# Order of work at the routes and gates of a two-layer diffusion trunk with product-key experts

## What is computed

```python
qr = (tb @ w_q).reshape(t, PEER_HEADS, 2, half)
s = jnp.einsum('thsk,hsnk->thsn', qr, sub_keys).astype(jnp.float32)
top_s, top_i = lax.top_k(s, PEER_TOPK)
cand_s = top_s[:, :, 0, :, None] + top_s[:, :, 1, None, :]
...
best_s, best_j = lax.top_k(cand_s.reshape(t, PEER_HEADS, PEER_TOPK * PEER_TOPK), PEER_TOPK)
gate = jax.nn.softmax(best_s, axis=-1)
act = jax.nn.gelu(jnp.einsum('td,thkd->thk', tb, expert_u[idx]).astype(jnp.float32), approximate=False)
w = (gate * act).astype(tb.dtype)
return jnp.einsum('thk,thkd->td', w, expert_v[idx])
```

## Time and profile before

| | us |
|---|---|
| median of 3 runs | 2819.0 |
| runs | 2814.79, 2819.0, 2820.88 |
| span of the profiled execution | 2820.7 |
| TensorE busy | 2637.5 (94%) |
| VectorE busy | 2261.6 (80%) |
| ScalarE busy | 1200.1 (43%) |
| GpSimd busy | 481.4 (17%) |

### The profile page before, as it was taken

The page is one execution under the profiler, slowest core; times in us unless marked ns, Lnnn a source line. Parts: engine busy times, 40 slices in busy tenths (PEclk is TensorE's granted clock), DMA queues, the critical chain, the costliest instruction groups (busy, mean ns, idle before and its releaser), DMA issues.

```text
span 2820.7 us, 48606 instructions
## 1 busy us (share of the span) xinstructions
PE 2637.5 (94%) x16753; PEld 2298.8 (81%) x16753; DVE 2261.6 (80%) x4592; ACT 1200.1 (43%) x2187; POOL 481.4 (17%) x432
## 2 busy tenths in 40 slices
PE   7999999775899999999999998989889999999998
PEld 5878877554788888888888887877879888888887
DVE  6487654996999999999999997786679888877776
ACT  5343432223954444444444445324425533333332
POOL 0000000002633333333333330000003211110010
PEclk9999999886999999999999999999999999999999
DMA  6532322643279999999999993333354599999985
GB/s 275 211 94 79 116 90 90 238 181 141 108 298 367 382 386 390 386 386 385 383 362 367 366 362 122 128 98 105 108 179 151 180 334 345 338 337 335 324 320 210
DMA packets 170928, 709.42 MB, mean 252 GB/s; under 512 B 17056, under 2 KB 48960, under 8 KB 123328
## 3 DMA queue, kind: packets, MB, share of 16 engines
q1 hardware_dynamic: 132464, 430.02, 41.3%
q0 software_dynamic: 38352, 277.92, 26.6%
HBM read 691.13 MB, written 16.65 MB: 251 GB/s over the span
## 4 chain that ended last, share of the span: by engine, by line
PE 83%; DVE 9%; DMA 3%; ACT 3%; issue 1%; SPq 0%; DVEq 0%; ACTq 0%; POOL 0%
PE ps L937 82%; DMA ring<-in_w_mod 2%; DVE hot L2685 1%; DVE hot L2680 1%; DMA gate_scratch<-spill 1%; DVE hot L2683 1%; DMA ring<-in_w_front 1%; DVE rs L2132 0%; DVE gst L2387 0%; DVE elo L2167 0%; PE ps L1085 0%; DVE loP L2232 0%; ACT hiP L1607 0%; DVE elo L2179 0%; DVE hx L2398 0%
## 5 line engine op out<-in xcount | busy, mean ns | idle before, releaser
L859 POOL DMA_INDIRECT gbuf<-in_expert_rows,gidx x192 | 277.4, 1445 | 1097.4 <-DVE yg L2738 1080.7
L937 PE MATMUL ps<-h2a,ehi 128*128 128x320 f32 x2048 | 455.0, 310 | 1.4 <-DVE elo L2695 1.4
L2084 ACT ACTIVATE ehi<-ring 128x1024 fp32r<-128x1024 f32 x256 | 271.1, 1059 | 394.5 <-PE ps L937 290.8
L2750 DVE TENSOR_TENSOR elo<-ring,ehi 128x1024 fp32r<-128x1024 f32 x256 | 313.6, 1225 | 136.2 <-ACT ehi L2084 132.9
L937 PE MATMUL ps<-ehi,wA 128*128 128x512 f32 x1280 | 375.3, 391 | 0.0
L937 PE MATMUL ps<-h2b,ring 128*128 128x192 f32 x2048 | 360.7, 327 | 1.0 <-ACT act_ahead L1969 1.0
L937 PEld LDWEIGHTS ps<-h2a,ehi 128*128 128x128 f32 x2048 | 349.3, 189 | 12.0 <-DVE elo L2695 1.9
L937 PEld LDWEIGHTS ps<-h2b,ring 128*128 128x128 f32 x2048 | 339.2, 191 | 10.6 <-issue 1.3
L937 PE MATMUL ps<-h2a,elo 128*128 128x320 f32 x1024 | 317.4, 310 | 0.0
L937 PEld LDWEIGHTS ps<-ehi,wA 128*128 128x128 f32 x1280 | 235.0, 188 | 49.8
L2728 DVE SCALAR_TENSOR_TENSOR gbuf<-gbuf,h2n 128x1024 f32<-128x1024 f32 x192 | 234.2, 1220 | 30.5 <-DMA gbuf<-in_expert_rows,gidx 25.3
(11 more groups left out here) (441 smaller groups left out, 4850.3 us busy)
## 6 DMA issues: line engine op xcount, KB each, us to landing
ring<-in_experts SPq DMA_DIRECT2D x512, 512.0 KB
ring<-in_w_mod SPq DMA_DIRECT2D x48, 1024.0 KB
ring<-in_w_side SPq DMA_DIRECT2D x24, 1024.0 KB
ring<-in_w_front SPq DMA_DIRECT2D x12, 1024.0 KB
ring<-in_w_merge SPq DMA_DIRECT2D x16, 768.0 KB
ring<-in_w_q SPq DMA_DIRECT2D x12, 1024.0 KB
gate_scratch<-spill SPq DMA_DIRECT2D x40, 256.0 KB, 2.1
gateA<-gate_scratch SPq DMA_DIRECT2D x16, 640.0 KB, 8.7
```

What stands on the lines that cost most here:

```text
L859: pool.indirect_dma_start(gbuf[:, k % 2, :], None, a[f"expert_rows{l}"], bass.IndirectOffsetOnAxis(gidx[:, at:at + 1], 0)).then_inc(gather ...
L937: return pe.matmul(out, w, x, start=start, stop=stop, **k)
L2084: act.activation(ehi[:, 2 + k % 2, :], ring[:, (u + k) % RING, DM:2 * DM], ACT.Copy).then_inc(vhi_ready, 1)
L2750: v.tensor_tensor(elo[:, r, DM:2 * DM], ring[:, r, DM:2 * DM], ehi[:, 2 + b, :].bitcast(F32), ALU.subtract).then_inc(vlo_ready, 1)
```

## The change

It reorders instructions and adds waits where the new order needs them; no product, copy or transfer is added or left out.

- SyncE, gates of layer 0: each of the first eight spills is followed by one of the eight opening half loads. In layer 1 the opening loads alternate, input half and output half of a slot.
- GpSimd, gates of layer 0: the first two gathers go out at group 40, the first "more" gather at group 48.
- TensorE: a wait for the fifth set of modulation tables in the query pass of route (0,0); the last of the 14 steps ahead comes behind the transposes of the picks, and its GELU at group 1 of the gates.
- ScalarE, route (0,0): exponent and index cast ahead of the two row copies. End of the gates of layer 0: the high part of the first expert's input half ahead of the last copies of gates.
- VectorE, route (0,1): the norm of the context tokens ahead of the two sets of modulation tables.

```diff
 # SyncE: opening loads of the experts, now only layer 1 calls this
                 for k in range(RING):
                     load_in(l, k)
-                for k in range(RING):
                     load_out(l, k)
...
 # SyncE, gates of layer 0, after the four index copies
-                    experts_begin(l)
-                    with sp.Fori(0, dense_tokens(l) // 16) as i:
+                    for m in range(2 * RING):
+                        count(sp, gate_ready, gb + 2 * m + 2)
+                        sp.dma_start(a["gate_scratch"][m], spill[:, m % 2, :, :]).then_inc(spill_out[m % 2], 16)
+                        (load_in if m < RING else load_out)(l, m % RING)
+                    with sp.Fori(0, dense_tokens(l) // 16 - RING) as i:
                         for b in range(2):
 
-                            count(sp, gate_ready, i * 4 + (gb + 2 * b + 2))
-                            sp.dma_start(a["gate_scratch"][bass.ds(i * 2 + b, 1)].rearrange("o p n t -> (o p) n t"),
+                            count(sp, gate_ready, i * 4 + (gb + 4 * RING + 2 * b + 2))
+                            sp.dma_start(a["gate_scratch"][bass.ds(i * 2 + (2 * RING + b), 1)].rearrange("o p n t -> (o p) n t"),
                                          spill[:, b, :, :]).then_inc(spill_out[b], 16)
...
 # GpSimd; gather_more itself only moves from the experts stage to ahead of the loop over stages
-                        if n == 4:
+                        if n == (4 if l else 40):
 
                             if l == DEPTH - 1:
                                 pool.wait_ge(shift_in, 32)
                             for m in range(2):
                                 gather(l, m)
+                        if n == 48 and not l:
+                            pool.wait_ge(more_in, 32 * SLOTS)
+                            gather_more(0)
...
                     if not l:
-                        pool.wait_ge(more_in, 32 * SLOTS)
-                        gather_more(0)
                         pool.wait_ge(more_moved, 1)
                         gather_more(1)
...
 # TensorE, queries(k)
                                 pe.wait_ge(head_copied, p + 1)
+                                if h == 0:
+
+                                    pe.wait_ge(mod_done, 5)
...
 # TensorE, route
-                    if l == DEPTH - 1:
-                        pe.wait_ge(h2_ready, 1)
-                        for j in range(IN_ROUTE):
+                    def ups_ahead(j0, j1):
+
+                        for j in range(j0, j1):
...
+                    if l == DEPTH - 1:
+                        pe.wait_ge(h2_ready, 1)
+                        ups_ahead(0, IN_ROUTE - 1)
                     pe.wait_ge(pick_ready, p + 1)
...
                     last.then_inc(pick_ps, 1)
+                    if l == DEPTH - 1:
+                        ups_ahead(IN_ROUTE - 1, IN_ROUTE)
...
 # TensorE, gates of layer 1
-                        pe.wait_ge(ahead_act, IN_ROUTE)
+                        pe.wait_ge(ahead_act, IN_ROUTE - 1)
                         for n in range(dense_tokens(l) // 4):
+                            if n == 2:
+
+                                pe.wait_ge(ahead_act, IN_ROUTE)
                             group(n, 0)
...
 # ScalarE, route; picks_in holds the exponent and the cast that stood behind ahead_out(0, AHEAD_EXP)
+                    def picks_in(p=p):
+
+                        act.wait_ge(exp_in, p + 1)
+                        act.activation(best[:, :, :, :], best[:, :, :, :], ACT.Exp).then_inc(exp_out, 1)
+                        act.activation(topf[:, :, :, :, :].rearrange("p s k t h -> p (t h) s k"),
+                                       topi[:, :, :, :].rearrange("p t (h s) k -> p (t h) s k", s=2), ACT.Copy).then_inc(topf_ready, 1)
+
+                    if st == ("route", 0, 0):
+                        picks_in()
                     if not h or l == DEPTH - 1:
                         act.wait_ge(rows_ps, l + 1)
                         act.activation(h2n[:, :], ps[:, 4:6, :].rearrange("p b d -> p (b d)"), ACT.Copy)
...
                         ahead_out(0, AHEAD_EXP)
...
+                    if st != ("route", 0, 0):
+                        picks_in()
...
-                        ahead_out(AHEAD_EXP, IN_ROUTE)
+                        ahead_out(AHEAD_EXP, IN_ROUTE - 1)
...
 # ScalarE, gates
+                    def u_high(k):
+
+                        v_ = BASE[("experts", l, 0)] + k
+                        act.wait_ge(u_in[v_ % RING], 16)
+                        act.activation(ehi[:, k % 2, :], ring[:, v_ % RING, 0:DM], ACT.Copy).then_inc(uhi_ready, 1)
+
...
+                        if l and n == 1:
+                            v_ = BASE[("route", l, 1)] + WQ_UNITS + mod_units(("route", l, 1)) + IN_ROUTE - 1
+                            unit_used(act, v_)
+                            act.activation(act_ahead[:, IN_ROUTE - 1, :], ps[:, 6 + (IN_ROUTE - 1) % 2, 0:192], ACT.Gelu).then_inc(ahead_act, 1)
...
+                    if not l:
+                        act.wait_ge(x_held, 16)
+
+                        count(act, gate_ps, gb + ng - 3)
+                        u_high(0)
                     columns(ng - 2)
...
 # ScalarE, experts
                     if not l:
-                        u_high(0, 0)
                         u_high(1, 0)
...
 # VectorE, route
                     if next_route(st):
+                        normed(next_route(st), rs2, 256, h2T, 0, lambda k, s: gain[:, l, 1, k, s:s + 1], h_scaled)
                         mod_tables(0, 5, 6, ps[:, 3, 10 * KD:12 * KD], 4)
                         mod_tables(1, 0, 2, ps[:, 2, 0:4 * KD], 5)
-                        normed(next_route(st), rs2, 256, h2T, 0, lambda k, s: gain[:, l, 1, k, s:s + 1], h_scaled)
```

More of the change, by code:

```diff
@@ L860, in gather, with gather_more @@
                                         bass.IndirectOffsetOnAxis(gidx[:, at:at + 1], 0)).then_inc(gather_in[k % 2], 16)
+            def gather_more(j):
+                pool.indirect_dma_start(gbufX[:, j % 2, :], None, a["expert_rows0"],
+                                        bass.IndirectOffsetOnAxis(gidx2[:, j:j + 1], 0)).then_inc(more_rows[j % 2], 16)
             for st in stages:
@@ L898, in _ @@
                 elif kind == "experts":
-                    def gather_more(j):
-                        pool.indirect_dma_start(gbufX[:, j % 2, :], None, a["expert_rows0"],
-                                                bass.IndirectOffsetOnAxis(gidx2[:, j:j + 1], 0)).then_inc(more_rows[j % 2], 16)
                     if not l:
-                        pool.wait_ge(more_in, 32 * SLOTS)
-                        gather_more(0)
                         pool.wait_ge(more_moved, 1)
@@ L1972, in _ @@
                         ahead_out(0, AHEAD_EXP)
-                    act.wait_ge(exp_in, p + 1)
-                    act.activation(best[:, :, :, :], best[:, :, :, :], ACT.Exp).then_inc(exp_out, 1)
-                    act.activation(topf[:, :, :, :, :].rearrange("p s k t h -> p (t h) s k"),
-                                   topi[:, :, :, :].rearrange("p t (h s) k -> p (t h) s k", s=2), ACT.Copy).then_inc(topf_ready, 1)
+                    if st != ("route", 0, 0):
+                        picks_in()
                     if next_route(st):
```

## The result

The changed kernel takes 2786.57 us in the median of 4 runs (2785.41 to 2789.01), the kernel before 2817.92 in the median of its 4 beside them (2814.79 to 2820.88): a ratio of 0.9884, interval 0.9873 to 0.9896. By the medians that is 31.4 us, by the ratio 32.7. The forecast was 2786.1. The profiled execution took 2787.19 us with a span of 2785.2, so the two profiles differ by 35.5 us. In every run of this study whose span is listed the time is about 2.0 us above it; by that (an estimate) the profiled execution of the kernel before took some 2822.7 us, more than any of its four timed runs.

The account below looks back on a forecast made before the run. TensorE bounds both expert loops and VectorE layer 0's gates, so gains lie in idle time between loops. Terms -3.7 - 12.4 - 10.7 + 1.5 - 2.0 - 2.1 - 3.5 = -32.9 give 2786.1 us from the median; range 2777 to 2799.

Parts of the forecast that it names:

- Norm first: Second query pass of layer 0: norm ahead of modulation tables lets queries follow TensorE's columns, -3.7 us (0 to -4.0).
- Picks: Route (0,0): exponent and index cast ahead of row copies remove VectorE's wait for the cast, -12.4 us (-11 to -12.5).
- tie of three engines: End of route (0,0): TensorE's row transposes at 657.6, ScalarE's copy at 658.66 and pick transposes at 658.6 finish nearly together.
- Gate stage: Layer 0 gates: loads behind spills recover 10.7 us, late gathers leak 1.5 (0 to 6), net -9.2 us.
- End of the stage: End of layer 0 gates: first up step 3.3 us earlier, first down step and loop gain 2.0 (0 to -3.3).
- both loops as long as before: Sign of being right: the expert loops of both layers keep their lengths, 922 and 574 us.
- Route (1,1): End of layer 1's route: one up step behind the pick transposes, its time hidden, -2.1 us (-1.5 to -2.1).
- Experts of layer 1: Start of layer 1's experts: alternating loads let ScalarE copy the first output half earlier, -3.5 us (-2.5 to -4.5).
- Rival A: Layer 0 gates: the stall moves to groups 40 and 48, leak 4 to 8 us, 2789 to 2793; chance 0.20.
- B: Route of layer 0 gives less: modulation weights hold TensorE's old times, about 2793 us (2790 to 2797); chance 0.14.
- C: Layer 0 expert loop settles at a gather's pace and not TensorE's, slower from 0.3 us a turn; chance 0.03.
- D: The change fails to do what it says, for instance a wait behind the hoisted cast, 2798 to 2815; chance 0.04.

Follow-up runs that it names:

- the second profile: The changed kernel run again without further edits, against the kernel before: 2787.6 us median of 4 runs, ratio 0.9881.

## Why the prediction was right

1. **Norm first, -3.7.** -3.99 in the profile pair, -3.98 alone. The queries are bound by the columns as said, and the wait before the key matmul cost nothing. By itself the edit is worth 5.4 us, because it moves a second chain, on which VectorE still waits as long as the picks are not moved.
2. **Picks, -12.4.** -12.43 and -12.42. The tie of three engines was real for this edit alone, and in the whole change it depends on the execution: TensorE's picks wait 3.63 and 2.91 us for VectorE in its two profiles, where the column products ran in part at full clock, and not at all where they took their 10.40 us. The stretch is 14.2 us either way.
3. **Gate stage, -9.2 net.** -8.63 and -10.18 in the two profiles, -9.1 from the mean of the four old stages (110.26) to that of the six new ones (101.14). The stage's 100.2 to 101.8 us and ScalarE's waits of 1.5 to 2.7 us came as forecast, VectorE's 0.8 to 2.3 us around the 1.5. Two steps behind the number were off. "Lands in its usual 2.0 us" is wrong for the spills among the loads (median 3.8), without a cost. And the prediction took the 10.7 us as one thing, which the trace of before could not divide: the order of the loads carries it, and the late gathers, a cost in the prediction, bring nothing for it once the loads are in order.
4. **End of the stage, -2.0.** The start of the down steps moved by -2.58, inside the bounds, but the step that failed is "both loops as long as before". The prediction counted when the first down step comes and not what TensorE does ahead of it: counted from the last hot group the up steps came 3.9 us earlier and the down step 2.6, half clock followed the stop between them (3.48 us), and the loop took back 1.46. Net -1.1, not -2.0.
5. **Route (1,1), -2.1.** -2.11, -2.02 and -2.00.
6. **Experts of layer 1, -3.5.** -3.54, -3.56 and -3.54, and 1.2 to 1.5 more in the loop, full clock in place of half. The prediction saw the copy and the wait rightly, and had no term for the clock here either. This gain and the loss in part 4 nearly cancel by luck, so the sum of -32.9 left both out and still met -33.1 in the stretches (-34.5 with the second profile) and -31.2 to -33.5 in the timed runs. That the median lies within 0.5 us of the forecast is more than the working could promise.

Rival A happened at its place, but at 0.8 to 2.3 us and not 4 to 8; B, C and D did not: queries began right behind the columns, the loop settled at TensorE's 7.14 us a turn of an expert tile, and VectorE has no idle time before the cast's product.

## What to carry to other kernels

Cut every trace at the same instructions and compare stretches, not spans: with the same edits most of them repeated within 0.3 us (the gate stage within 1.6), where spans of one kernel differed by several. Before a wait of TensorE, or for TensorE, is put down to an edit, compare the granted clock of the same instructions in a second profile: 2.7 us came and went with it in two places here. When the head of a pipeline is moved earlier, move its next link with it; a stop between the two can cost the clock as well as its length. Work that VectorE put off once came back at the next step; put off by one place in every step, it cost nothing here, where VectorE has half a microsecond to spare per step.

## What was not expected of the hardware

- At the start of the two loops TensorE had full clock behind stops of 0.84, 0.94, 1.42 and 1.44 us; half clock for part of the first 5 us behind 1.76, in each of six profiles behind 3.5 and in each of four behind 4.5 to 4.8; and behind 2.08 once half and once full. Half clock there cost 1.2 to 1.7 us.
- TensorE's 48 column products of the second query pass took 10.40 us at a granted clock of 0.50 and 7.66 at 0.70; nothing waited for the difference in the changed kernel.
- Stretches with the same instructions differed between executions by up to 5.8 us (331.23 and 325.45), and the one from yout to the next norm took 15.8, 17.4 or 19.0 us and nothing between.
- Two gathers of 1 MB and a burst of eight loads ahead of one spill cost VectorE 10.67 us, the burst without the gathers 5.52, the gathers with one load behind each spill 0.58: far from a sum.
